# Expert layer on one core: 48 tokens by gathered rows in place of 32, 208 tokens dense, 78 up columns ahead of the gates

## What is computed

```python
def block(xb):                      # 128 tokens at a time
    q = (xb @ w_query).reshape(PEER_TOKEN_BLOCK, PEER_HEADS, 2, D_KEY // 2)
    s = jnp.einsum('thpc,pkc->thpk', q, sub_keys).astype(jnp.float32)
    ...
    e = (jnp.take_along_axis(i1, ci // PEER_TOPK, axis=-1) * N_KEYS
         + jnp.take_along_axis(i2, ci % PEER_TOPK, axis=-1))
    g = jax.nn.softmax(sc, axis=-1)
    u = expert_u[e]
    act = jax.nn.gelu(jnp.einsum('td,thkd->thk', xb, u).astype(jnp.float32))
    return jnp.einsum('thk,thkd->td', (g * act).astype(xb.dtype), expert_v[e])
```

## Time and profile before

| | us |
|---|---|
| median of 3 runs (lowest, highest) | 1224.87 (1224.71, 1226.81) |
| the profiled execution's own time | 1224.35 |
| its span, first to last instruction | 1222.6 |
| TensorE busy | 1197.8 (98%) |
| VectorE / ScalarE / GpSimd busy | 728.2 / 701.8 / 737.8 |
| mean granted TensorE clock | 0.998 of full speed |

### The profile page before, as it was taken

How to read it: one execution, slowest core, us unless ns; L and a number is a source line. 1 busy time by engine, 2 the same in 40 slices (tenths; PEclk the granted TensorE clock), 3 DMA queues, 4 the chain that set the end, 5 groups by cost and what they waited for, 6 DMA issues and landing times.

```text
span 1222.6 us, 24119 instructions
## 1 busy us (share of the span) xinstructions
PE 1197.8 (98%) x8853; PEld 1126.1 (92%) x8853; DVE 728.2 (60%) x1482; ACT 701.8 (57%) x1369; POOL 737.8 (60%) x357
## 2 busy tenths in 40 slices
PE   7999999999999999999999999999999999999997
PEld 6788999999999999999999999999999888899886
DVE  3454049994007788885677777777548642357423
ACT  5585445556548887875555555555464555546554
POOL 7747868888997777777601122221067766677654
PEclk9999999999999999999999999999999999999999
DMA  6735445555455445447678777777474343354332
GB/s 242 258 121 190 173 138 192 203 204 198 173 203 184 164 166 179 157 170 271 206 235 274 263 274 272 274 272 265 172 260 156 139 138 137 137 195 151 132 131 103
DMA packets 66888, 237.66 MB, mean 194 GB/s; under 512 B 8592, under 2 KB 10104, under 8 KB 66432
## 3 DMA queue, kind: packets, MB, share of 16 engines
q1 hardware_dynamic: 57024, 206.14, 48.7%
q0 software_dynamic: 7648, 25.73, 5.7%
q10 hardware_dynamic: 2144, 4.85, 1.1%
HBM read 232.30 MB, written 6.31 MB: 195 GB/s over the span
## 4 chain that ended last, share of the span: by engine, by line
PE 89%; POOL 3%; DMA 3%; ACT 2%; DVE 2%; issue 1%; SPq 0%; DVEq 0%; ACTq 0%
PE W L574 28%; PE W L818 8%; PE A L818 8%; PE A L820 4%; PE W L820 4%; PE A L618 4%; PE A L625 4%; PE A L620 4%; PE A L598 3%; PE A L603 3%; PE A L599 3%; POOL ringl L485 3%; PE W L857 2%; PE A L751 1%; PE A L746 1%; PE A L748 1%
## 5 line engine op out<-in xcount | busy, mean ns | idle before, releaser
L485 POOL TENSOR_TENSOR ringl<-ring,ringh 128x1024 fp32r<-128x1024 f32 x263 | 639.6, 2442 | 226.1 <-ACT ringh L1112 130.4
L574 PE MATMUL W<-XTh,ringh 128*128 128x256 f32 x1024 | 287.8, 281 | 2.1 <-POOL ringl L485 2.0
L574 PE MATMUL W<-XTl,ringh 128*128 128x256 f32 x1024 | 282.9, 276 | 0.0
L574 PE MATMUL W<-XTh,ringl 128*128 128x256 f32 x1024 | 282.8, 276 | 0.0
L1112 ACT ACTIVATE ringh<-ring 128x1024 fp32r<-128x1024 f32 x135 | 141.7, 1057 | 142.3 <-PE A L603 45.5
L1301 ACT ACTIVATE ringh<-ring 128x1024 fp32r<-128x1024 f32 x180 | 189.0, 1050 | 10.8 <-DMA ring<-exp_v 9.5
L574 PEld LDWEIGHTS W<-XTh,ringh 128*128 128x128 f32 x1024 | 192.4, 188 | 2.5 <-ACT H L1244 2.2
L574 PEld LDWEIGHTS W<-XTl,ringh 128*128 128x128 f32 x1024 | 192.5, 188 | 0.0
L574 PEld LDWEIGHTS W<-XTh,ringl 128*128 128x128 f32 x1024 | 192.2, 188 | 0.0
L1741 DVE TENSOR_TENSOR ringl<-ring,ringh 128x1024 fp32r<-128x1024 f32 x127 | 155.6, 1225 | 58.0 <-ACT ringh L1301 57.2
L818 PE MATMUL W<-HP,ringh 128*128 128x448 f32 x512 | 170.1, 366 | 0.2 <-DVE HP L1746 0.2
(11 more groups left out here) (298 smaller groups left out, 2191.0 us busy)
## 6 DMA issues: line engine op xcount, KB each, us to landing
ring<-exp_u SPq DMA_DIRECT2D x128, 512.0 KB, 3.2
ring<-exp_v SPq DMA_DIRECT2D x128, 512.0 KB, 3.8
ring<-w SPq DMA_DIRECT2D x72, 512.0 KB, 3.2
ring<-w_out SPq DMA_DIRECT2D x24, 512.0 KB, 3.2
ring<-w_in SPq DMA_DIRECT2D x20, 512.0 KB, 4.4
ring<-w_query SPq DMA_DIRECT2D x16, 512.0 KB, 3.1
skewed<-scratch POOLq DMA_DIRECT2D x1, 2048.0 KB, 10.6
H<-lng POOLq DMA_DIRECT2D x2, 1024.0 KB, 7.2
```

The costliest lines, as they stand in the source:

```text
L485: pool.tensor_tensor(ringl[:, slot, :], ring[:, slot, :], ringh[:, slot, :].bitcast(F32), ALU.subtract)\
L574: last = pe.matmul(dst, stationary[a], moving[b], start=start and n == 0, stop=stop and n == 2, skip_group_check=True)
```

## The change

The tail grows from 32 to 48 tokens, in two sets. The first set is the last 32 tokens in 4 groups (32 gathers), the second is the 16 tokens before them in 8 groups (16 gathers); each set has its own sum buffer in ACC, its own index and gate tiles, and its own SEL. So there are 48 gathers and 48 fetches of activations. There are four gather slots, and one tile is added after every second column, from column 27 to column 121. TD is 208: 52 rounds of gates, 416 in place of 448 columns in the first matmul of a down chunk, and still 256 in the second (208 values and 48 zeros). 78 up columns stand ahead of the gates and 50 in their rounds. The index and gate tiles of the second set come by 16 small DMAs from ScalarE's queue, two after each of the columns 60 to 67. The fold is 16 products and stands behind column 126.

```diff
-TD = 224
+TD = 208
-U_AHEAD = 75
+U_AHEAD = 78
...
-FOLD_AT = TURN_AT + 2
+FOLD_AT = TURN_AT + 4
-FIRST_COLUMN = [7, 6, 0, 1, 3, 5, 2, 4]
-GROUPS = P // TS
-GATHERS = NK // GROUPS
-GATHER_SLOTS = 3
-FIRST_ADDED = 26
+FIRST_COLUMN = [7, 6, 0, 1, 2, 4, 3, 5]
+SETS = ((32, TD + 16), (16, TD))
+GATHERS = sum(n for n, _ in SETS)
+GATHER_SLOTS = 4
+FIRST_ADDED = 27
...
-    k, r = divmod(col - FIRST_ADDED, 3)
+    k, r = divmod(col - FIRST_ADDED, 2)
...
-        ACC = place(D)
+        both = place(2 * D)
+        ACC = both.rearrange("p (n d) -> p n d", n=2)
...
-            pool.wait_ge(idx_in, 16 * GROUPS)
+            pool.wait_ge(idx_in, 16 * 4)
+            pool.wait_ge(idx2_in, 16 * 8)
             for g in range(GATHER_SLOTS):
                 gather(g)
             pool.wait_ge(tail_out[0], 16 * 5)
             pool.wait_ge(tail_out[1], 16 * 4)
-            for g in range(GATHERS):
-                pool.indirect_dma_start(ZD[:, g:g + 1], None, bass.AP(tail_h.tensor, 0, [[1, P * NK * TS], [1, 1]]),
-                                        bass.IndirectOffsetOnAxis(IDX[:, 1, g:g + 1], axis=0)).then_inc(zd_in, 16)
+            for n, (picks, _) in enumerate(SETS):
+                for j in range(picks):
+                    pool.indirect_dma_start(ZD[n][:, j:j + 1], None, bass.AP(tail_h.tensor, 0, [[1, P * NK * TS], [1, 1]]),
+                                            bass.IndirectOffsetOnAxis(IDX[n][:, 1, j:j + 1], axis=0)).then_inc(zd_in, 16)
...
                     pe.wait_ge(gath_used, GATHERS)
-                    for c in range(KC):
-                        pe.matmul(DOWN[c][:, 2 * TD:HP_END], ACC[:, c * P:(c + 1) * P], SEL, start=False, stop=False,
-                                  skip_group_check=True)
+                    for n, (tokens, at) in enumerate(SETS):
+                        for c in range(KC):
+                            pe.matmul(DOWN[c][:, TD + at:TD + at + tokens], ACC[:, n, c * P:(c + 1) * P], SEL[n],
+                                      start=False, stop=False, skip_group_check=True)
...
             for col in range(BEFORE_PICKS, U_AHEAD - SLOTS):
                 ahead(col)
+                n, first = SETS[1]
+                at = slice(first - P, first - P + n)
+                if LOWS_BEFORE_PICKS <= col < LOWS_BEFORE_PICKS + 4:
+                    act.wait_ge(idx_set, 1)
+                    for q in range(2 * (col - LOWS_BEFORE_PICKS), 2 * (col - LOWS_BEFORE_PICKS) + 2):
+                        act.dma_start(IDX[1][q * n:(q + 1) * n, :, :], E[at, :, q * n:(q + 1) * n]).then_inc(idx2_in, 16)
+                if LOWS_BEFORE_PICKS + 4 <= col < LOWS_BEFORE_PICKS + 8:
+                    act.wait_ge(pick_ready, NB)
+                    for q in range(2 * (col - LOWS_BEFORE_PICKS - 4), 2 * (col - LOWS_BEFORE_PICKS - 4) + 2):
+                        act.dma_start(GQ[1][q * n:(q + 1) * n, :], PICK[at, 2, 1, q * n:(q + 1) * n]).then_inc(gq2_in, 16)
...
                 if g == 0:
-                    dve.wait_ge(gq_in, 16 * GROUPS)
+                    dve.wait_ge(gq_in, 16 * 4)
+                    dve.wait_ge(gq2_in, 16 * 8)
                     dve.wait_ge(zd_in, 16 * GATHERS)
-                    step(dve.tensor_tensor(GA, ZD, GQ, ALU.mult))
+                    for a in range(2):
+                        dve.tensor_tensor(ZD[a], ZD[a], GQ[a], ALU.mult).then_inc(zd_gated, 1)
+                    dve.wait_ge(zd_gated, 2)
```

More of the change, by code:

```diff
@@ L305, in program @@
         GATED_HOT = halves[:, 2 * 4 * P:2 * 4 * P * (1 + GATE_PARTS)].rearrange("p (s n a e) -> p s n a e", s=2, n=4, a=GATE_PARTS)
-        at[0] = 60 * TD
+        at[0] = 55 * TD
         QT = place(4096).rearrange("p (n t) -> p n t", n=2 * NH)
@@ L323, in program @@
         GATHERED = [place(D) for _ in range(GATHER_SLOTS)]
-        ACC = place(D)
-        TAIL = ACC[:, 0:2 * STAGE * TS].rearrange("p (s c t) -> p s c t", s=2, c=STAGE)
+        both = place(2 * D)
+        ACC = both.rearrange("p (n d) -> p n d", n=2)
+        TAIL = both[:, 0:2 * STAGE * TS].rearrange("p (s c t) -> p s c t", s=2, c=STAGE)
         EF, E = GATHERED[1][:, 0:P], GATHERED[2].bitcast(U32)[:, 0:2 * P].rearrange("p (a n) -> p a n", a=2)
-        IDX = RB[:, 0:64].bitcast(U32).rearrange("p (a n) -> p a n", a=2)
-        ZD, GQ, GA, SEL = (RB[:, 32 * n:32 * n + 32] for n in range(2, 6))
+        IDX = [RB[:, 0:64].bitcast(U32).rearrange("p (a n) -> p a n", a=2),
+               RB[:, 64:96].bitcast(U32).rearrange("p (a n) -> p a n", a=2)]
+        ZD, GQ, SEL = ([RB[:, a:a + 32], RB[:, a + 32:a + 48]] for a in (96, 144, 192))
         tail_h = nc.dram_tensor("tail_h", (P, NK * TS), F32, kind="Internal").ap()
@@ L383, in program @@
         h_final, xt_kept, v_done, v_back, end_gain = (sem(n) for n in ("h_final", "xt_kept", "v_done", "v_back", "end_gain"))
-        idx_set, idx_in, gq_in, tail_set, zd_in = (sem(n) for n in ("idx_set", "idx_in", "gq_in", "tail_set", "zd_in"))
+        idx_set, idx_in, gq_in, tail_set, zd_in, zd_gated = (sem(n) for n in (
+            "idx_set", "idx_in", "gq_in", "tail_set", "zd_in", "zd_gated"))
+        idx2_in, gq2_in = sem("idx2_in"), sem("gq2_in")
         tail_out = [sem(f"tail_out{n}") for n in range(2)]
@@ L513, in _ @@
             pool.wait_ge(idx_set, 1)
-            for q in range(GROUPS):
-                pool.dma_start(IDX[q * TS:(q + 1) * TS, :, :], E[P - TS:P, :, q * GATHERS:(q + 1) * GATHERS]).then_inc(idx_in, 16)
+            n, first = SETS[0]
+            for q in range(P // n):
+                pool.dma_start(IDX[0][q * n:(q + 1) * n, :, :], E[first - P:first - P + n, :, q * n:(q + 1) * n])\
+                    .then_inc(idx_in, 16)
             pool.wait_ge(pick_ready, NB)
-            for q in range(GROUPS):
-                pool.dma_start(GQ[q * TS:(q + 1) * TS, :], PICK[P - TS:P, 2, 1, q * GATHERS:(q + 1) * GATHERS])\
+            for q in range(P // n):
+                pool.dma_start(GQ[0][q * n:(q + 1) * n, :], PICK[first - P:first - P + n, 2, 1, q * n:(q + 1) * n])\
                     .then_inc(gq_in, 16)
@@ L815, in down @@
                     f = slice(m * P, (m + 1) * P)
-                    if first and m == 2:
+                    if first and m == 3:
                         pe.wait_ge(col_done, AMID)
@@ L1309, in _ @@
             ahead_high(U_AHEAD - 1)
-            act.wait_ge(gq_in, 16 * GROUPS)
+            act.wait_ge(gq_in, 16 * 4)
+            act.wait_ge(gq2_in, 16 * 8)
             for q in range(QUADS):
@@ L1619, in _ @@
                                 (W4, A4)[tb][:, 2:4, :].rearrange("p a b -> p (a b)")).then_inc(keys_dve, 1)
-            dve.tensor_reduce(SEL, ident.rearrange("p (q i) -> p i q", q=GROUPS), AX.X, ALU.add)
+            for n, (tokens, _) in enumerate(SETS):
+                dve.tensor_reduce(SEL[n], ident.rearrange("p (q i) -> p i q", i=tokens), AX.X, ALU.add)
             dve.wait_ge(rest_in, 16)
@@ L1751, in add_gathered @@
                 dve.wait_ge(gath_in[g % GATHER_SLOTS], 16 * (g // GATHER_SLOTS + 1))
-                rows_in, gate = GATHERED[g % GATHER_SLOTS], GA[:, g:g + 1]
+                n, j = divmod(g, SETS[0][0])
+                rows_in, gate, acc = GATHERED[g % GATHER_SLOTS], ZD[n][:, j:j + 1], ACC[:, n, :]
                 if g == 0:
-                    dve.wait_ge(gq_in, 16 * GROUPS)
+                    dve.wait_ge(gq_in, 16 * 4)
+                    dve.wait_ge(gq2_in, 16 * 8)
                     dve.wait_ge(zd_in, 16 * GATHERS)
-                    step(dve.tensor_tensor(GA, ZD, GQ, ALU.mult))
+                    for a in range(2):
+                        dve.tensor_tensor(ZD[a], ZD[a], GQ[a], ALU.mult).then_inc(zd_gated, 1)
+                    dve.wait_ge(zd_gated, 2)
+                if j == 0:
+                    dve.tensor_scalar(acc, rows_in, gate, None, ALU.mult).then_inc(gath_used, 1)
                 else:
                     dve.wait_ge(gath_used, g)
-                if g == 0:
-                    dve.tensor_scalar(ACC, rows_in, gate, None, ALU.mult).then_inc(gath_used, 1)
-                else:
-                    dve.scalar_tensor_tensor(out=ACC, in0=rows_in, scalar=gate, in1=ACC, op0=ALU.mult, op1=ALU.add)\
+                    dve.scalar_tensor_tensor(out=acc, in0=rows_in, scalar=gate, in1=acc, op0=ALU.mult, op1=ALU.add)\
                         .then_inc(gath_used, 1)
```

5 lines of the change are left out of this document (3 added, 2 removed).

## The result

| | before | changed |
|---|---|---|
| median of 4 runs, side by side (lowest, highest), us | 1225.84 (1224.71, 1241.52) | 1255.36 (1247.96, 1259.28) |
| ratio to before, 95% interval | | 1.0212 (1.0163 to 1.0262) |
| profiled execution: time, span, us | 1224.35, 1222.6 | 1259.28, 1257.5 |

What follows compares the result with a forecast made beforehand. TensorE was taken to bound the kernel, the down stage by its matmuls. Terms -13.7 - 2.1 - 2.2 + 1.7 + 2.4 + 0.6 = -13.3 gave 1211.6 us, range 1207.8 to 1219.5.

Steps and rivals of the forecast that it cites:

- Gathers beside the loads: Down stage from column 29: denser loads and gathers fit at 321 GB/s, costing TensorE only +0.6 us.
- My second rival: Down stage: gathers make loads late repeatedly, at one gather in three, 9.6 us in place of 0.6: 1220.6 us; chance 0.15.
- The first rival: Down stage from column 29: DMA engines sustain no more than 262 GB/s, +49 us: 1260 us; chance 0.04.
- The down matmuls: Down stage: first matmul of each chunk 448 to 416 columns at 0.42 ns each, -13.7 us (-11 to -16.5).
- Gates: Gate stage: four rounds fewer, -2.1 us, and the stall at the end of the gates gone, -2.2 us.
- the first down column: Start of down stage: its low part of H is ready in time, covered by 0.5 us.
- The fold: Fold behind column 126: 16 products instead of 8, priced per product, +1.7 us.
- The wait for the fetches: Near column 30, VectorE waits 2.8 us at its first add, TensorE 2.5; with the first rush +2.4 us together.
- the first rush: Early down stage: a fourth gather delays loads, +2.0 us (0 to 2.3), not added to the fetch wait; larger counts.
- No price: Terms put at zero: sixteen small DMAs on ScalarE's queue, GpSimd's 8 small DMAs, wider tail and narrower dense tiles.

Runs made afterwards that it cites:

- the denser pace: Kernel before with an add and gather at every second column instead of every third: 1242.47 us, ratio 1.0117; an earlier run on a slower chip, 1.0076.
- the fourth buffer: Changed kernel with its fourth gather slot made a fourth buffer for f32 weights in down columns 24 to 119: 1220.86 us, ratio 0.9943.
- the run again: Changed kernel measured once more, no edit, beside the kernel before on the same chip: 1252.49 us, ratio 1.0185.
- The fetches cut to two: Changed kernel fetching only the first element of each set as the gate of all its rows: 1247.39 us, ratio 1.0140.
- the version with both cures: Changed kernel with a fourth weight buffer and the first add at column 29 instead of 27: 1216.94 us, ratio 0.9898; on a slower chip 1.0011.
- small gathers: Changed kernel with gathers from the fifth on fetching 32 values per row instead of 1024, adds whole: 1224.12 us, ratio 0.9983.
- short adds: Changed kernel adding only 32 of 1024 columns, first add of each set and gathers whole: 1275.08 us on a slower chip, ratio 1.0169.

## Why the prediction was wrong

Between the forecast (-13.3) and the two spans (+34.9) lie 48 us: 38.3 in the down stage (-9.0 forecast, +29.3 measured), 7.0 ahead of it, 3.0 behind it.

**The step that failed is "Gathers beside the loads", +0.6 us.** It measured 17.7 us of stops over 640 to 880 us in the profiled execution and 20.0 in the next, and some 8 to 14 us more that come with them. Four things were wrong in it.
- I took 7 us from issue to landing for "where the cover of the three ring slots ends", and 0.3 us off it for the shorter columns. The 7 us were right for the kernel before: its longest load stops TensorE for 0.18 us.

```profile
675.32 7.23 DMA ring<-exp_v
```

```profile
685.24 0.47 PE L818 MATMUL W<-HP,ringh 128*128 128x448 f32 x1 [0.18 <-DVE HP L1746]
```

  In the changed kernel the load of 6.91 us brings a stop of 1.63, and the longest, of 7.59, one of 2.25: its cover ends at 5.3 us (6.91 - 1.63 and 7.59 - 2.25). Of the 1.7 to 1.8 us that are gone, 0.35 is ScalarE's lead (5.2 before, 4.87 now), by the three shorter columns, and 1.28 is the add. The kernel before with the denser pace bears this out: its columns are not shorter, a load of 7.13 us at 717.65 brings a stop of 1.37, and so its cover ends at 5.8 us, which is the 7.05 of before (7.23 - 0.18) less the 1.28 of the add.
- I priced the next such load by the 0.25 us that it had cost before. What it costs hangs on what is queued behind it on VectorE. At a pace of three that is the low part of H, at a pace of two an add and then the low part of H. This follows from the order of the work alone.
- Twice 0.25 and 0.3 are 0.8 and not 0.6; this changes nothing.
- I sized the adds at about 0.9 us from the gap behind the first one, but the first is a plain product. The other 31 take 1.28 us each in the trace of before.

My second rival had the mechanism (loads late again and again) and was priced at one gather in three and 0.6 us each. Measured over 640 to 880 us, in 42 gathers: 10 stops of 1.8 us on the mean, and 15 of 1.3 in the next execution. The count was fair, the size too small by two to three times, and the clock was left out. The first rival, DMA engines that can't carry it, falls by the fourth buffer: 304 GB/s without a stop.

**The clock.** I had it in no term. After the wait at the first add TensorE runs at the lower of its two levels while its own work is back to full:

```profile
636.00:637.00 1.00, 1.00 (x6) 0.98 (x5) 1.00 (x3) 0.00 (x0) 0.98 (x1) 0.68 0.00 0
637.00:638.00 1.00, 1.00 (x6) 0.97 (x5) 1.00 (x2) 0.00 (x0) 0.00 (x0) 0.50 0.69 127
638.00:639.00 1.00, 1.00 (x5) 0.98 (x4) 0.77 (x1) 0.00 (x0) 0.00 (x0) 0.50 0.66 205
```

Over the down stage: +29.3 = -10.9 (columns) + 1.8 (fold) + 22.3 (waits, less the 0.2 of before) + 16.1 left. The low clock makes about 13 of these, by an estimate from the clock of the windows: 9 to 10 over 640 to 880 us (0.96), some 2 around 637 (0.83 over 630 to 640) and some 2 around 892 (0.83 over 890 to 900). Some 3 us I can't assign. In the run again it is +26.0 = -10.9 + 1.8 + 25.8 + 9.3 left, at a clock of 0.99 over 640 to 880. The stop of 1.63 us at 663 shows no lower clock behind it, so a stop does not always bring one.

**The down matmuls, -13.7.** A column measures 2.47 us, not 2.45:

```profile
598.07 0.35 PE L827 MATMUL W<-HP,ringh 128*128 128x416 f32 x1
...
600.54 0.35 PE L827 MATMUL W<-HP,ringh 128*128 128x416 f32 x1
```

Against 2.56 that is -10.9 with 2.475 over the stage (my bound was -11). I had taken 0.42 ns a column from a step between starts that are printed to 0.01 us, and they could not carry it.

**Gates, -2.1 and -2.2.** The stall of the earlier trace rows is gone, as forecast:

```profile
551.93 1.07 PE L866 MATMUL W<-X 128*128 128x128 f16 x16
...
556.45 0.43 PE L827 MATMUL A<-HP,ringh 128*128 128x416 f32 x1 [0.57 <-DVE HP L1768]
```

The last two rounds run without a wait. But the first down column is not covered by 0.5 us, as I had put it; it is 0.57 late. In the run again the gate stage is 11.8 us shorter and the stage ahead of it 10.1 longer, net -1.7 in place of -4.3; two of the missing us are TensorE's pace ahead of the gates. In the profiled execution the two are 6.8 shorter and 9.8 longer, net +3.0. Here the gate stage takes 169.0 us, in the run again 164.1, and in neither does TensorE wait but for its last 0.6 and 0.7 us. It makes the matmuls at another pace, before, changed, and changed again:

```profile
400.00:530.00 130.00, 130.00 (x1284) 128.58 (x1283) 106.71 (x281) 104.89 (x321) 95.30 (x41) 1.00 0.49 169
```

```profile
400.00:530.00 130.00, 130.00 (x1246) 128.32 (x1245) 102.71 (x272) 101.96 (x311) 92.80 (x39) 1.00 0.51 164
```

```profile
400.00:530.00 130.00, 130.00 (x1285) 128.57 (x1284) 106.36 (x280) 105.14 (x321) 95.32 (x41) 1.00 0.53 171
```

So 5 of the 7 us that the profiled execution is off ahead of the down stage are this pace, which is no matter of the change (last section). That the forecast of the gates comes near in the run again is no proof of its terms, since the pace alone moves it by more than them.

**The fold, +1.7**: 913.73 to 917.22, 3.49 us in place of 1.70. Right.

**The wait for the fetches, +2.4.** Right in place and nearly in size; VectorE and TensorE:

```profile
633.67 0.28 DVE L1781 TENSOR_TENSOR RB<-RB 128x32 f32<-128x32 f32 x2 [3.77 <-DMA RB<-tail_h,RB]
...
635.08 0.46 PE L827 MATMUL W<-HP,ringh 128*128 128x416 f32 x1 [3.06 <-DVE HP L1768]
```

2.8 and 2.5 forecast. The last fetch begins at 629.90, 73.4 us after the stage (72.2 forecast), and VectorE goes on at 633.67, 3.8 us later. By the Trainium skill (DMA: Bandwidth & Descriptors, Anatomy of one DMA), which puts a DMA issued by GpSimd at about 2.0 us plus bytes / 436 GB/s, it would have been free at an estimated 631.9; the trace disagrees by 1.8 us. With the clock behind it, it costs 4 to 5 us: 3.06 of wait and some 1.7 of low clock by the trace. The fetches cut to two gave 5 and the later first add 3.9, neither clear of noise by itself. No stop came in the first rush.

**No price.** ScalarE's 16 small DMAs held up nothing: ahead of the gates TensorE has the one wait of 2.0 us that it had before. With the stops and the fetch wait away the sum can be tried: without the 2.4 it says -15.7, and the version with both cures stands at 1216.94 - 1227.75 = -10.8 on one chip. Of the 4.9 between them 2.8 are the columns and 0.6 the first down column. The interval of that ratio is 7 us to either side, and on another chip the version gained nothing, so this fits the ledger but does not prove it. What it does not cover is the pace and the clock of TensorE.

## What to carry to other kernels

Before a queue is made fuller, work out the lead of the critical loads, from issue to the start of the engine that wants them, and what the engines behind it hold in reserve. Hold the two together against the longest load in the trace, not the median. Then look at what stands in the in-order queue behind the engine that such a load holds up: a change of pace (three to two) can put a long instruction there every time. When loads are late but the bytes fit, one more buffer can buy as much as leaving out the bytes did (here 0.9943 and 0.9983 of the kernel before, with intervals that overlap).

## What the runs showed of the hardware

- A load of 512 KB takes 3.4 to 4.6 us in this stage beside the small gathers, and up to 7.6 us in the changed kernel, 8.3 in its second run, when a gather of 128 rows of 4 KB is under way from the second queue, at a DMA share of 0.81 and 0.80. With one load more in flight the stage carries 304 GB/s, and the median load takes 6.5 us.
- TensorE's pace has two values at granted clock 1.00. Over 200 to 330 us, in which it makes the same 256-column matmuls without a gap, it is 1149 of them in the changed kernel and 1106 in the run with small gathers, where nothing is different up to there:

```profile
200.00:330.00 130.00, 130.00 (x1149) 130.00 (x1148) 88.68 (x273) 69.70 (x148) 115.30 (x50) 1.00 0.61 201
```

```profile
200.00:330.00 130.00, 130.00 (x1106) 130.00 (x1106) 85.64 (x267) 66.90 (x143) 110.62 (x47) 1.00 0.60 194
```

  The distance between starts is 0.113 or 0.1175 us; it changes between executions and within one. The kernel before shows both too: 1150 matmuls there in the profile ahead of the prediction, 1106 in the earlier run with the denser pace. Over this stage of some 220 us it is worth up to 8 us, more than most terms of the sum, and the granted clock does not tell it.
- GpSimd needs 0.94 us to issue a gather, and 1.97 when VectorE's split of a weight tile is already running as it begins, as at 651.04 us above, with the split from 650.97. That is so in 32 of the 42 gathers over 640 to 880 us; in the other ten the split begins behind the gather's start or there is none, and they take 0.94 to 1.11. Beside short adds the split is less often ahead, and the mean is 1.18 us (40 in 47.05) in place of 1.71 (42 in 71.76). The Trainium skill (SBUF - State Buffer, Who interferes with whom) says that GpSimd's writing of descriptors is starved where VectorE takes the port that both share, and that who issues first keeps it. But it has a tensor_tensor take only the read side, which by its own inference the writing of descriptors does not need. The split is a tensor_tensor, so the trace does not fit that inference. VectorE never waits for a gathered tile in the changed kernel, so it cost nothing here.
